# Attention values with stationary weights, two products fewer for decays and lengths, and a held ring load

## The reference

```python
def swiglu(x, w_gu, w_down):
    gate, up = jnp.split(x @ w_gu, 2, axis=-1)
    return (jax.nn.silu(gate) * up) @ w_down          # 1024 -> 2 x 2816 -> 1024

def memory_attention(q, mem_kv):                      # 4 heads of 64, 256 memory tokens
    k, v = ...split(mem_kv)...
    sc = jnp.einsum("bqhd,bmhd->bhqm", q, k) * 64 ** -0.5
    p = jax.nn.softmax(sc, axis=-1)
    return jnp.einsum("bhqm,bmhd->bqhd", p, v).reshape(b, s, 256)

# layer 0
x = x + 0.5 * swiglu(rms_norm(x), ...)
x = x + concat([gated_deltanet(...), memory_attention(q_mem, mem_n @ w_mem_kv[0])]) @ w_out[0]
x = x + 0.5 * swiglu(rms_norm(x), ...)
...                                                   # latent keys and values
# layer 1
x = x + 0.5 * swiglu(rms_norm(x), ...)
q = rms_norm(cq, b_q_norm) @ b_w_uq                   # cq: 256 columns of the latent query
x = x + concat([mla_attention(...), memory_attention(q_mem, mem_n @ w_mem_kv[1])]) @ w_out[1]
x = x + 0.5 * swiglu(rms_norm(x), ...)
# second block: a hybrid mixer, then x = x + (silu(h @ w_gate) * (h @ w_up)) @ w_down
```

## Time and profile before

| | before |
|---|---|
| median of 3 runs | 1273.53 us (1272.91 to 1276.81) |
| profiled execution | 1275.8 us |
| its span | 1274.0 us |
| granted TensorE clock | 1.0, of 2.4 GHz |
| busy TensorE, VectorE, ScalarE | 99%, 78%, 66% of the span |
| TensorE's weight loads, beside its products | 83% |
| moved by DMA | 331.90 MB, 261 GB/s |

### The profile page before, as it was taken

The page is one execution under the profiler, slowest core; times in us unless marked ns, Lnnn a source line. Parts: engine busy times, 40 slices in busy tenths (PEclk is TensorE's granted clock), DMA queues, the critical chain, the costliest instruction groups (busy, mean ns, idle before and its releaser), DMA issues.

```text
span 1274.0 us, 17252 instructions
## 1 busy us (share of the span) xinstructions
PE 1261.1 (99%) x6904; PEld 1056.8 (83%) x6904; DVE 988.3 (78%) x1140; ACT 840.9 (66%) x1083; POOL 68.3 (5%) x100
## 2 busy tenths in 40 slices
PE   9999999999999999999999999999999999999998
PEld 7888888889988887887787888888888898888877
DVE  5887777778558888786478867679887798698885
ACT  7676658766556666586466666666666857776663
POOL 0000000000000000000000000000000100000000
PEclk9999999999999999999999999999999999999999
DMA  9997648887686798868688786768899988867772
GB/s 351 312 329 225 239 160 287 278 265 222 180 285 257 267 301 294 309 220 254 229 292 306 227 268 183 265 262 248 299 313 288 318 253 252 327 213 263 264 242 74
DMA packets 49279, 331.90 MB, mean 261 GB/s; under 512 B 5484, under 2 KB 7788, under 8 KB 10160
## 3 DMA queue, kind: packets, MB, share of 16 engines
q1 hardware_dynamic: 34512, 230.88, 47.3%
q0 software_dynamic: 13536, 97.27, 30.9%
q10 hardware_dynamic: 1152, 2.66, 0.6%
HBM read 329.73 MB, written 65.02 MB: 310 GB/s over the span
## 4 chain that ended last, share of the span: by engine, by line
PE 76%; DMA 7%; issue 7%; DVE 7%; ACT 2%; POOL 0%; SPq 0%; POOLq 0%; ACTq 0%; DVEq 0%
PE ps L2916 19%; PE ps L2918 19%; PE ps L2917 19%; PE ps L2826 7%; DMA arena<-in_tiles 6%; DVE w_lo_part L1761 4%; PE ps L3049 2%; ACT w_hi_part L702 1%; DMA made_sums<-in_tiles 1%; PE ps L2937 1%; PE ps L2945 1%; PE ps L2950 1%; PE ps L570 1%; PE ps L2842 1%; PE ps L572 1%
## 5 line engine op out<-in xcount | busy, mean ns | idle before, releaser
L1761 DVE TENSOR_TENSOR w_lo_part<-w_raw,w_hi_part 128x2048 fp32r<-128x2048 f32 (+2 forms) x181 | 409.2, 2265 | 51.2 <-ACT w_hi_part L702 50.4
L702 ACT ACTIVATE w_hi_part<-w_raw 128x2048 fp32r<-128x2048 f32 (+1 forms) x180 | 341.3, 1897 | 86.6 <-PE ps L2918 67.2
L2916 PE MATMUL ps<-w_hi_part,x_hi 128*128 128x512 f32 (+1 forms) x680 | 267.8, 394 | 0.8 <-DVE w_lo_part L1761 0.5
L2918 PE MATMUL ps<-w_hi_part,x_lo 128*128 128x512 f32 (+1 forms) x680 | 258.9, 381 | 0.0
L2917 PE MATMUL ps<-w_lo_part,x_hi 128*128 128x512 f32 (+1 forms) x680 | 258.3, 380 | 0.0
L702 ACT ACTIVATE w_hi_part<-arena 128x2048 fp32r<-128x2048 f32 x78 | 148.5, 1914 | 86.4 <-DMA arena<-in_tiles 49.8
L1761 DVE TENSOR_TENSOR w_lo_part<-arena,w_hi_part 128x2048 fp32r<-128x2048 f32 x78 | 177.4, 2288 | 29.5 <-ACT w_hi_part L702 29.0
L2916 PE MATMUL ps<-w_hi_part,h_hi_part 128*128 128x512 f32 x464 | 183.9, 396 | 0.0
L2918 PE MATMUL ps<-w_hi_part,h_lo_part 128*128 128x512 f32 x464 | 181.0, 390 | 0.0
L2917 PE MATMUL ps<-w_lo_part,h_hi_part 128*128 128x512 f32 x464 | 180.8, 390 | 0.0
L2918 PEld LDWEIGHTS ps<-w_hi_part,x_lo 128*128 128x128 f32 x680 | 127.9, 188 | 25.1
(11 more groups left out here) (458 smaller groups left out, 1609.7 us busy)
## 6 DMA issues: line engine op xcount, KB each, us to landing
w_raw<-in_tiles SPq DMA_DIRECT2D x176, 1024.0 KB, 7.1
made_sums<-in_tiles POOLq DMA_DIRECT2D x60, 1024.0 KB, 8.9
arena<-made_sums SPq DMA_DIRECT2D x30, 1024.0 KB, 8.2
arena<-in_tiles POOLq DMA_DIRECT2D x21, 1024.0 KB, 11.1
arena<-in_tiles SPq DMA_DIRECT2D x9, 1024.0 KB, 7.6
mem_kv<-in_tiles POOLq DMA_DIRECT2D x6, 1024.0 KB, 10.6
w_raw<-in_tiles SPq DMA_DIRECT2D x3, 512.0 KB, 6.0
arena<-in_w_ukv POOLq DMA_DIRECT2D x1, 1536.0 KB, 8.6
```

The costliest lines, as they stand in the source:

```text
L702: nc.scalar.activation(WH[:, n % RING, 0:w], source(n), ACT.Copy).then_inc(S["w_hi"], 1)
L1761: nc.vector.tensor_tensor(WL[:, n % RING, 0:w], source(n), WH[:, n % RING, 0:w], ALU.subtract).then_inc(S["w_split"], 1)
L2916: nc.tensor.matmul(o, a_hi, w_hi, start=start, stop=False, skip_group_check=True)
L2918: return nc.tensor.matmul(o, a_lo, w_hi, start=False, stop=stop, skip_group_check=True)
```

## The change

In both memory attentions the values become the stationary operand (64 columns) and the turned probabilities of a head move (256 columns). Two heads are made by one call, the one on the lower half of the array's columns and PSUM's partitions, the other on the upper half. The result then has the layout that the output projection wants, so the four transposes at the end and the buffers `OM`, `OM1` go. The division by the row sums moves ahead of the turn (`m0_normed`, `m1_normed`), where queries are on partitions. The decays of both token blocks are summed by one product; the squares of the latent query are added by VectorE first. VectorE's `w_lo` of tile 18 moves behind the sums of the reads. In the four quads the ring load of `m2` of each pair but the first of a layer waits until t4 of the pair before it has landed.

Line numbers below are those of the diff's hunks; renumbered semaphore waits on ScalarE and in `ml_turn` are left out.

```diff
@@ SP, the ring
+                if n in kind_of and kind_of[n][0] in QUADS and kind_of[n][1] == "m2" and kind_of[n][2] > steps_of(kind_of[n][0])[0]:
+                    sp.wait_ge(*t4_added(kind_of[n][0], kind_of[n][2] - 2))
                 w = width(n)
                 sp.dma_start(RAW[:, r % RING, 0:w], d["tiles"][t, :, 0:w]).then_inc(w_loaded[r % RING], 16)
@@ VectorE
+            def m0_normed(u):
+                c = slice(2 * u, 2 * u + 2)
+                dve.wait_ge(S["att_e"], u + 1)
+                link(nc.vector.reciprocal(M0RC[:, c], M0SUM[:, c]))
+                nc.vector.tensor_tensor(M0S[u % 2], M0S[u % 2], M0RC[:, c].unsqueeze(2).broadcast_to([P, TB, SEQ]),
+                                        ALU.mult).then_inc(S["att_p"], 1)
@@
             m0_maxima(1)
+            m0_normed(0)
             query_decay(2)
             level_inverse(5)
-            w_lo(n0 + 18)
+            m0_normed(1)
@@
             m0_maxima(3)
+            m0_normed(2)
...
+            m0_normed(3)
@@
-            dve.wait_ge(S["m0_v"], MH)
-            link(nc.vector.reciprocal(M0RC, M0SUM))
...
-            last.then_inc(S["m0_om"], 1)
+            w_lo(n0 + 18)
@@ layer 1 (the removed OM1 as above; m1_normed as m0_normed, on M1S, from att_e at MH + u + 1)
             m1_maxima(0)
+            m1_normed(0)
@@
             m1_maxima(1)
             m1_turned(0)
+            m1_normed(1)
             w_lo(n0 + 3)
             m1_maxima(2)
             m1_turned(1)
+            dve.wait_ge(S["lat_sq"], 1)
+            nc.vector.tensor_tensor(LSQ[:, 0, :], LSQ[:, 0, :], LSQ[:, 1, :], ALU.add).then_inc(S["lat_sq"], 1)
             m1_maxima(3)
+            m1_normed(2)
@@
             rotate(0)
+            m1_normed(3)
             m1_turned(2)
             w_lo(n0 + 4)
             m1_turned(3)
@@ TensorE
-                for tb in range(TB):
-                    f32mm(PS[:, 7, AH * tb:AH * tb + AH], con("tri"), GG[:, AH * tb:AH * tb + AH])
+                f32mm(PS[:, 7, 0:2 * AH], con("tri"), GG[:, 0:2 * AH])
@@
             def m0_turn(u):
-                pe.wait_ge(S["att_e"], u + 1)
+                pe.wait_ge(S["att_p"], u + 1)
@@
-            def m0_values(u):
-                pe.wait_ge(S["att_pt"], u + 1)
-                if u == 0:
+            def m0_values(j):
+
+                pe.wait_ge(S["att_pt"], 2 * j + 2)
+                if j == 0:
                     pe.wait_ge(S["vb_sb"], 5)
-                for q in range(TB):
-                    for kb in range(TB):
-                        last = f32mm(bank(0)[:, q * SEQ + 64 * u:q * SEQ + 64 * u + 64], M0P[u % 2][:, kb, q * P:(q + 1) * P],
-                                     MEM_V[0][:, kb, 64 * u:64 * u + 64], kb == 0, kb == TB - 1)
+                for kb in range(TB):
+                    for i, r in enumerate(HALVES):
+                        u = 2 * j + i
+                        last = f32mm(PS[r, 0, j * SEQ:(j + 1) * SEQ], MEM_V[0][:, kb, 64 * u:64 * u + 64], M0P[i][:, kb, :],
+                                     kb == 0, kb == TB - 1)
                 last.then_inc(S["m0_v"], 1)
@@ latent_lengths
-                pe.wait_ge(S["lat_sq"], 1)
+                pe.wait_ge(S["lat_sq"], 2)
                 for tb in range(TB):
-                    for b in range(2):
-                        last = f32mm(PS[:, 4, tb:tb + 1], LSQ[:, b, tb * P:(tb + 1) * P], con("ones", 0, 1), b == 0, b == 1)
+                    last = f32mm(PS[:, 4, tb:tb + 1], LSQ[:, 0, tb * P:(tb + 1) * P], con("ones", 0, 1))
@@ the order of layer 1 (m1_turn waits for att_p at MH + u + 1; m1_values as m0_values, in bank 7)
             query_block(0, 1, bank(0)[:, SEQ:]).then_inc(S["uq_ps"], 1)
-            m1_values(0)
             m1_scores(1)
             m1_turn(1)
...
-            m1_values(1)
+            m1_values(0)
             latent_lengths()
...
-            m1_values(2)
...
             ml_scores(0)
-            m1_values(3)
+            m1_values(1)
             swap(1)
             bias_product()
             swap(2)
-            pe.wait_ge(S["m0_om"], 2)
...
             ml_scores(1)
```

## The result

| | before | changed |
|---|---|---|
| median of 6 runs | 1273.87 us (1272.91 to 1276.81) | 1278.70 us (1277.41 to 1279.36) |
| ratio of the runs | | 1.0029, 95% interval 1.0019 to 1.0039 |
| profiled execution, its span | 1275.8, 1274.0 us | 1278.37, 1276.6 us |

A forecast was written before the change was run, and what follows sets the result against it. TensorE was taken to bound the kernel, busy 99% of the 1274.0 us span. Layer 0 -1.1, layer 1 -0.3 and the hold -0.8 gave -2.2 us, so a median of 1271.3; range 1266.5 to 1276.5.

The forecast's parts named there:

- rival (b): Quads: p3, third in a row behind the held m2, lands too late for t2; +3.9 us, 1277.4; chance 0.12.
- The attention's work: Both attentions, TensorE work without waits: 1.07 us per two heads, 2.14 for 3.36 a layer, 3.9 us saved in all.
- Layer 0: Attention of layer 0 with its waits: values save 1.22 us, last group loses 0.2, last transposes save nothing; -1.1 us.
- 1.22 less 0.2: Layer 0 attention: values of heads 0 to 3 save 1.22 us, the last group loses 0.2.
- the 0.21 us of the decays: Layer 0 attention: gain of the decays, 0.21 us, eaten because `query_decay(2)` is 0.7 us late and the keys' turn waits.
- Layer 1: Attention of layer 1 with its waits: 0.3 us gained at `m1_scores(1)`, `m1_values` waiting for late copies; -0.3 us.
- the late copies: Layer 1 attention: VectorE's last copies ready at 768.3 and 777.2, TensorE at `m1_values` at 767.6 and 776.7.
- The hold: Quads' later pairs, m2's load held for t4: turn waits change by -2.3 us, GpSimd's copies and adds +1.5; -0.8 us.
- t2 starts 17.9 us after t4's issue: Quads' eleven later places: t4 8.0 us, then 0.1, then p3 landing 9.8 later, which sets t2's start at 17.9.
- 1.5 us for all disturbances: Quads: GpSimd's copies and adds start about when p3 streams, at eight places, some 0.2 us each; +1.5 us.
- at best the present wait gone: Quads' eleven turns: each place's gain is limited to its present wait; changes from -1.2 to +0.6 us, sum -2.3.
- the 4.3 us that were to be recovered: Quads' eleven later turns of hidden values: TensorE's lost time before the change, 4.3 us in all, all gone at best.

The follow-up runs named there:

- e11: Kernel without the hold and with t2 moved behind `hidden`, upper head of each two left out of both attentions' values; 1288.15 us, its parent 1289.51.

## Why the prediction was wrong

I forecast 1271.3 with 0.58 for no difference, and 0.12 for slower. It became slower, and in the main by the mechanism of rival (b): p3, third behind the held m2, was late for t2.

**The attention's work was right in size:** 1.07 us forecast for a group of two heads, 1.02 measured, halves at once (e11). So a layer's values fell from 3.36 to 2.04 us. The Trainium skill (TensorEngine Tiling (Array Packing), Theoretical Speedup) has up to 2x for a dimension of 64 or less, 1.68 us here as an estimate; measured were 2.04. The pairing itself is complete. Eight steps of 0.216 us are 1.73 us; the other 0.3 us lie at the two ends of each group, where the first step takes 0.267 and the next product starts 0.31 after the last step's records.

**Layer 0** was forecast at -1.1 (its own terms, 1.22 less 0.2, add up to 1.0) and gave -1.3: `memory(3, 0)` waits 0.78 us, as I said, so the missing transposes are worth nothing there. `query_decay(2)` did start 0.6 us later with respect to TensorE, but the keys' turn did not, and the 0.21 us of the decays stayed gained.

**Layer 1** was forecast at -0.3 and gave -1.3. The query product and `m1_scores(1)` behaved as written (start 0.4 us sooner). The step that failed is that of the late copies: I had `m1_values` wait 0.7 and 0.5 us, it waited 0.3 and 0.1, and `rotate(1)` let `ml_scores(1)` go at once (row 781.68), since the 0.9 us of VectorE's old division no longer stood ahead of it and the last copy came 0.9 us sooner than I had it.

**The hold** was forecast at -0.8 and cost 5.4 us in the trace, 7.3 in the runs with and without it. The inputs of this step were good: t4 with m2 held takes mostly 7.7 to 8.1 us (8.0 forecast), and the loads land 4.9, 7.4 and 9.8 behind the landing (4.9, 7.3, 9.8). What failed is what was made of them. First, "t2 starts 17.9 us after t4's issue" was put in as one number, with 1.5 us for all disturbances. The traces taken together show that a turn loses time from a t2 of about 17.9 us on (18.0 gave 0.1, 18.9 gave 0.9), and from 17.4 at the first place of each layer (17.8 gave 0.4). So the expected t2 lay on the edge or just past it: what comes sooner gains nothing, what comes later costs all of it. With the hold on m2 and t2 in its old place the traces had t2 at 17.5 to 21.5. With this hold the t4 at s = 5 of ffn1 and ffn3 took 8.4 to 9.0 in all traces but one (8.0); at s = 7 of ffn4 m1 and p3 landed 1.3 to 1.5 us late in all but one. Second, "at best the present wait gone" was right as a bound, but the sum took -0.9, -0.6, -0.7 and -1.2 at the four longest waits, where the trace gave -0.8, -0.7, +0.5 and -0.5. Third, two consequences were not priced at all: the clock behind a long wait, 1.5 us in the trace, and the later copies of GpSimd, 1.2 to 2.0 us of wait at the bias copy in four of the traces with a hold (not in that of the first runs). Fourth, the 4.3 us that were to be recovered came from one execution. Without the hold three traces show 1.9, 2.2 and 2.9 us at the same eleven turns, so there was less to gain; whether before itself has 4.3 as a rule, one trace does not tell. Of the 6.2 us between the traces of the kernel timed again and of no hold again, each less its lag at the start, 4.7 are at the eleven turns and 1.1 at the bias copy. I had asked whether m2 and m1 were covered and not what else is queued behind them: the t3 load landed 21 to 27 us after t4's issue where it had been 17 to 20, with GpSimd's additions on the DMA engines beside it.

Rival (b) named the queue and the threshold of t4 at 8.6 us; the price of 1277.4 was near, its chance of 0.12 too small, since it was held against the mean of t4 and not against its spread: most t4 stayed under 8.6, and t2 was late at all eleven places even so.

**Open:** why the hold alone took 14 us, when before and no hold, timed beside it, took their usual times. Its one trace is of its fastest run, 1282.38; the slower ones have a lower mean granted clock (0.998 at 1285.91, 0.997 at 1292.31, 0.995 at 1292.82, against 0.999), so part of it is likely the clock behind long waits, but no trace shows which waits. Of the changed kernel's single run, 12 us over before, the place in ffn3 is the larger part. Also open is why single t4 take over 10 us with m2 held.

## What to carry to other kernels

Before a transfer is held, list what is queued behind it and the first engine that needs the last of these: holding three loads cost 7.3 us, two 2.7, and one 0.7, which is within the noise. Where two ends race, don't work with their means: at the edge every delay counts in full and every lead counts nothing, so price the spread. Take what there is to gain from more than one trace: 4.3 us of waits in one became 1.9 to 2.9 in three others. And before an instruction is moved off one wait in an in-order queue, walk the list on to every later item that inherits its time: here t2 moved three times and found a new wait of 0.7 to 1.6 us each time.

## What the runs showed of the hardware

- Beside a wait of TensorE of 2.46 us the granted clock was 0.50 for 3.4 us, from 0.6 us after the wait's end; beside one of 3.38 us for 6.8 us, from 0.7 us before its end. Products of 512 columns then stood 0.43 us apart where they are 0.23. After the waits of 1.83, 1.91 and 2.03 us in other traces there was no such stretch.
- The adding DMA of 1 MB took 7.7 to 9.4 us at the eleven places with m2 held, two of 10.2 and 10.6 apart, and 8.0 to 12.7 with m2, or m2 and m1, beside it.
- Products of 256 columns with 64 stationary ones run at once on the two column halves, alternating or not: four records in 1.01 us, eight in 1.02, in steps of 0.216 us.
